# The order of the first tile's work, of the sampled rows' loads and of the last sigmoid in a one-layer decoder kernel

## The reference

```
xn = rms_norm(x, norm_mix_g)                       # x * rsqrt(mean(x^2) + eps) * g
qa, ka, va, qr, kr, vr, gr, g_a, g_b = split(xn @ w_in)   # w_in: 1024 x 11264
oa = differential attention(qa, ka, va)            # 8 heads, prompt causal; sampled rows with a paged cache
or = retention(qr, kr, vr)                         # 4 heads, keys of 256, values of 512, chunks of 128
m  = sigmoid(g_a + b) * (norm(oa) @ w_pa) + sigmoid(g_b + b) * ((norm(or) * silu(gr)) @ w_pb)
h  = x + m @ w_o
y  = rms_norm(h + (silu(hn @ w_g) * (hn @ w_u)) @ w_down),  hn = rms_norm(h)
```

## Time and profile before

| | us |
|---|---|
| runs shown | 2793.14, 2794.50, 2794.54 |
| median | 2794.5 |
| the profiled execution's own time | 2795.3 |
| its span (first to last instruction) | 2793.4 |
| PE busy | 2750.4 (98%) |
| VectorE, GpSimd, ScalarE busy | 1280.7, 867.7, 719.3 |

### The profile page before, as it was taken

How to read it: one execution, slowest core, us unless ns; L and a number is a source line. 1 busy time by engine, 2 the same in 40 slices (tenths; PEclk the granted TensorE clock), 3 DMA queues, 4 the chain that set the end, 5 groups by cost and what they waited for, 6 DMA issues and landing times.

```text
span 2793.4 us, 41305 instructions
## 1 busy us (share of the span) xinstructions
PE 2750.4 (98%) x16146; PEld 2330.2 (83%) x16146; DVE 1280.7 (46%) x2465; ACT 719.3 (26%) x1518; POOL 867.7 (31%) x700
## 2 busy tenths in 40 slices
PE   7999999999999999999999999999999999999998
PEld 5888877777777778787777789999899999997886
DVE  5441255536556644554444442343375555542224
ACT  4111122225555532222121121011232222221011
POOL 3342522202211222221222233535023444455340
PEclk9999999999999999999999999999999999999999
DMA  4324256553343234456545454243122222244321
GB/s 138 123 79 149 95 191 203 201 180 114 100 131 122 85 124 156 161 183 194 184 159 176 156 200 142 102 148 134 68 88 70 70 81 82 70 154 156 91 60 64
DMA packets 277776, 362.11 MB, mean 130 GB/s; under 512 B 28514, under 2 KB 172514, under 8 KB 277602
## 3 DMA queue, kind: packets, MB, share of 16 engines
q1 hardware_dynamic: 277602, 359.74, 38.9%
HBM read 257.24 MB, written 111.35 MB: 132 GB/s over the span
## 4 chain that ended last, share of the span: by engine, by line
PE 93%; DVE 3%; ACT 2%; DMA 1%; issue 1%; SPq 0%; ACTq 0%; DVEq 0%
PE psum L521 22%; PE psum L1293 14%; PE psum L2647 14%; PE psum L2017 13%; PE psum L546 10%; PE psum L986 3%; PE psum L1012 2%; PE psum L2629 2%; PE psum L2050 2%; PE psum L2063 2%; PE psum L1970 1%; PE psum L2671 1%; PE psum L1407 1%; PE psum L1002 1%; PE psum L2056 1%
## 5 line engine op out<-in xcount | busy, mean ns | idle before, releaser
L351 POOL TENSOR_TENSOR w_h<-stage,ones 128x512 fp32r<-128x512 f32 x268 | 305.0, 1165 | 1347.0 <-PE psum L2017 419.5
L358 POOL TENSOR_TENSOR w_l<-stage,w_h 128x512 fp32r<-128x512 f32 x268 | 355.7, 1354 | 123.4 <-DVE acc L1134 118.7
L521 PE MATMUL psum<-w_h,xt_h 128*128 128x512 f32 x864 | 344.4, 399 | 5.9 <-DVE xt_l L492 3.1
L521 PE MATMUL psum<-w_h,xt_l 128*128 128x512 f32 x864 | 343.1, 397 | 0.0
L521 PE MATMUL psum<-w_l,xt_h 128*128 128x512 f32 x864 | 343.0, 397 | 0.0
L2017 PE MATMUL psum<-xt_h,w_h 128*128 128x384 f32 x744 | 289.1, 389 | 0.0
L2017 PE MATMUL psum<-xt_h,w_l 128*128 128x384 f32 x744 | 245.1, 329 | 0.0
L2017 PE MATMUL psum<-xt_l,w_h 128*128 128x384 f32 x744 | 245.0, 329 | 0.0
L401 POOL TENSOR_TENSOR w_l<-stage,w_h 128x512 fp32r<-128x512 f32 x106 | 139.2, 1313 | 268.6 <-ACT w_h L2741 268.6
L1293 PE MATMUL psum<-w_h,xt_h 128*128 128x512 f32 x512 | 218.0, 426 | 0.0
L1293 PE MATMUL psum<-w_l,xt_h 128*128 128x512 f32 x512 | 202.2, 395 | 0.0
(11 more groups left out here) (299 smaller groups left out, 5585.0 us busy)
## 6 DMA issues: line engine op xcount, KB each, us to landing
stage<-in_w_in_dram SPq DMA_DIRECT2D x88, 512.0 KB, 5.7
proj<-edge SPq DMA_DIRECT2D x112, 256.0 KB, 2.0
out_dram<-acc SPq DMA_DIRECT2D x44, 512.0 KB, 3.6
stage<-in_w_gu_dram SPq DMA_DIRECT2D x88, 256.0 KB, 3.8
acc<-proj SPq DMA_DIRECT2D x82, 256.0 KB, 3.1
gates<-edge SPq DMA_DIRECT2D x32, 544.0 KB, 4.1
acc<-in_cache_k_dram SPq DMA_DIRECT2D x32, 512.0 KB, 5.3
acc<-in_cache_v_dram SPq DMA_DIRECT2D x32, 512.0 KB, 4.6
```

Of the source, the lines that this page charges most:

```text
L351: last = nc.gpsimd.tensor_tensor(w_h[s][:, a:b, :], src, one.unsqueeze(1).to_broadcast([128, b - a, WN]), ALU.mult)
L358: last = nc.gpsimd.tensor_tensor(w_l[s][:, a:b, :], stage[h][:, a - lo:b - lo, :], w_h[s][:, a:b, :].bitcast(F), ALU.subtract)
L521: last = nc.tensor.matmul(psum[:, bank, :], x, w[s][:, k, :], start=k == 0 and n == 0, stop=k == nk - 1 and n == len(passes) - 1)
```

## The change

At the start, gain and identity are loaded ahead of the first weight half. VectorE makes the low pieces 5, 6 and 7 of the first weight tile (`BY_DVE`), counted on v_done, and GpSimd the other five. ScalarE makes the first half of rows 0's high part, w_h piece 0, the second half, and the other pieces. From row tile 3 on, square and root (ScalarE) and roots (VectorE) stand ahead of high and low part of the tile before. SP's loads of q and k for head 0 move to step 61 of the attention, behind a wait for the transposes of the last query half; PE waits for those two (32), VectorE for all five (80). `DN_PART` gives ScalarE and VectorE one row tile behind the second chunk instead of three; the others follow the last sigmoid, and VectorE's low parts stand `t + 3` ahead.

```diff
--- before.py
+++ after.py
@@ -114,7 +114,7 @@
 def v_step(n, name):
-    return sum(len(v_names(m)) for m in range(n)) + v_names(n).index(name) + 1
+    return len(BY_DVE) + sum(len(v_names(m)) for m in range(n)) + v_names(n).index(name) + 1
 def s_step(n, name):
@@ -124,7 +124,7 @@
 N_OPERANDS = operand(PAIRS)
-DN_PART = [(0, 2), (2, 5), (5, NT)]
+DN_PART = [(0, 2), (2, 3), (3, NT)]
 LAST_ORDER = [*range(NT - 2), SAMPLE, NT - 2]
@@ -133,12 +133,15 @@
     return banks_before(w) + (LAST_ORDER.index(t) if w == N_W - 1 else t)
-PIECES = 2 * KD - 4
+BY_DVE = [5, 6, 7]
+PIECES = 2 * KD - len(BY_DVE) - 4
 def split_count(w, h):
-    return KD * w + 4 * (h + 1) if w < 2 else PIECES + 2 * w + h + 1
+    if w == 0:
+        return 4 * (h + 1) - (len(BY_DVE) if h else 0)
+    return KD - len(BY_DVE) + 4 * (h + 1) if w == 1 else PIECES + 2 * w + h + 1
 def tile_no(w):
@@ -305,6 +308,8 @@
             sp.wait_ge(op_split, N_OPERANDS)
         elif w >= 1:
             sp.wait_ge(w_split, split_count(tile_no(w) - 1, h))
+            if (w, h) == (1, 1):
+                sp.wait_ge(v_done, len(BY_DVE))
         load_half(sp, w_source(w), h, W_NK[w])
     def load_w(sp, w):
@@ -351,7 +356,7 @@
                     last = nc.gpsimd.tensor_tensor(w_h[s][:, a:b, :], src, one.unsqueeze(1).to_broadcast([128, b - a, WN]),
                                                    ALU.mult)
                 last.then_inc(w_high, 1)
-                pool.wait_ge(w_high, no * 2 + (PIECES + h + 1))
+                pool.wait_ge(w_high, no * 2 + (2 * KD - 4 + h + 1))
                 for a, b in pairs:
                     if beat is not None:
                         pool.wait_ge(mix_ready, beat + (8 * h + 4 + a - lo) * 13 // 16 + 1)
@@ -366,6 +371,8 @@
         def first_low(w):
             for k in range(KD):
+                if w == 0 and k in BY_DVE:
+                    continue
                 pool.wait_ge(w_high, KD * w + k + 1)
                 nc.gpsimd.tensor_tensor(w_l[w][:, k, :], stage[k // 4][:, k % 4, :], w_h[w][:, k, :].bitcast(F),
                                         ALU.subtract).then_inc(w_split, 1)
@@ -472,8 +479,8 @@
     def transposed(tag, g, t):
         return psum[:, norm_banks[tag][2](g), :].rearrange("p (k n) -> p k n", k=4)[:, :, 0:rows(t)]
-    def act_high_tile(act, tag, t, place, xh, xs):
-        for b in range(2):
+    def act_high_tile(act, tag, t, place, xh, xs, bs=range(2)):
+        for b in bs:
             g = place(b)
             act.wait_ge(norm_banks[tag][0], g + 1)
             if t == SAMPLE:
@@ -506,7 +513,9 @@
             for k in ks:
                 if inside is not None and (t, k) in inside:
                     pe_norm_tile(pe, "mix", inside[t, k], lambda b: 2 * inside[t, k] + b)
-                if t == 0 and (pieces or k % 4 == 0):
+                if t == 0 and pieces and split == 1 and k in BY_DVE:
+                    pe.wait_ge(v_done, BY_DVE.index(k) + 1)
+                elif t == 0 and (pieces or k % 4 == 0):
                     pe.wait_ge(w_split, split + (k if pieces else k // 4))
                 state = ready(t, k) if ready is not None else None
                 if state is not None:
@@ -571,9 +580,9 @@
             sp.dma_start(x_rows[0:rows(t), t, :], token_rows(x_prompt, x_sample, t)).then_inc(x_loaded[x_group(t)], 16)
         load_x(0)
+        sp_load_gain(sp, norm_mix_g[0])
+        sp.dma_start(ident[:, :], c_ident).then_inc(ident_loaded, 16)
         load_half(sp, w_source(0), 0)
-        sp.dma_start(ident[:, :], c_ident).then_inc(ident_loaded, 16)
-        sp_load_gain(sp, norm_mix_g[0])
         load_half(sp, w_source(0), 1)
         for t in range(1, NT):
             load_x(t)
@@ -640,7 +649,7 @@
         inside = {(0, 7): 1, (1, 4): 2, (2, 2): 3, (2, 7): 4, (3, 4): 5, (4, 1): 6, (4, 6): 7, (5, 4): 8}
         for j in range(2):
-            pe_token_tile(pe, xt_h1, xt_l1, xs_hl1, j, KD * j + 1, lambda t: (G_TM + NT * j + t, (G_TM + NT * j + t) % RING),
+            pe_token_tile(pe, xt_h1, xt_l1, xs_hl1, j, (KD - len(BY_DVE)) * j + 1, lambda t: (G_TM + NT * j + t, (G_TM + NT * j + t) % RING),
                           ready=None if j else lambda t, k: (mix_free, 2 + 2 * t + k // 4 + 1) if k % 4 == 0 else None,
                           pieces=True, inside=None if j else inside)
         with pe.Fori(1, W_KR // 2) as i:
@@ -660,18 +669,24 @@
             act.wait_ge(x_loaded[x_group(t)], X_GROUPS[x_group(t)] * 16)
             act_square(act, "mix", x_rows, t)
-        def high_tile(t):
-            act_high_tile(act, "mix", t, lambda b: 2 * t + b, xt_h1, xs_hl1)
+        def high_tile(t, bs=range(2)):
+            act_high_tile(act, "mix", t, lambda b: 2 * t + b, xt_h1, xs_hl1, bs)
         act.wait_ge(ones_set, 2)
         nc.scalar.activation(rstd[:, 0:1], ones[:, :], ACT.Sqrt)
         square(0)
         act_deviation(act, "mix", 0)
-        first_high(0, range(KD))
+        high_tile(0, [0])
+        first_high(0, [0])
+        high_tile(0, [1])
+        first_high(0, range(1, KD))
         for t in range(1, NT):
-            high_tile(t - 1)
+            if t == 2:
+                high_tile(t - 1)
             square(t)
             act_deviation(act, "mix", t)
+            if t > 2:
+                high_tile(t - 1)
             if 4 <= t < 8:
                 first_high(1, [2 * (t - 4), 2 * (t - 4) + 1])
         high_tile(NT - 1)
@@ -707,11 +722,18 @@
             dve_low_tile(dve, "mix", t, lambda b: 2 * t + b, xt_h1, xt_l1, xs_hl1)
         for t in range(NT):
-            if t:
+            if 1 <= t <= 2:
                 low_tile(t - 1)
+            if t == 1:
+                for k in BY_DVE:
+                    dve.wait_ge(w_high, k + 1)
+                    nc.vector.tensor_tensor(w_l[0][:, k, :], stage[1][:, k - 4, :], w_h[0][:, k, :].bitcast(F),
+                                            ALU.subtract).then_inc(v_done, 1)
             dve_rstd(dve, "mix", t)
             if t == 0:
                 dve.wait_ge(gain_loaded, 16)
+            if t > 2:
+                low_tile(t - 1)
             dve_scale_tile(dve, "mix", x_rows, t)
         dve_att_constants(dve)
         low_tile(NT - 1)
@@ -936,6 +958,9 @@
                 load_w_half(sp, W_VR + n // 16 + 2, 0 if n % 16 == 8 else 1)
             if n % 3 == 2 and n // 3 < 2 * NT:
                 copy_rows(n // 3)
+            if n == STEPS - 3:
+                sp.wait_ge(x_full, x_index(X_LOADS[-1]) + 1)
+                sp_load_qk_inputs(sp, 0)
         store_half(2 * DH - 2)
         for n in (STEPS - 2, STEPS - 1, STEPS):
             for u in UNITS_OF[n]:
@@ -944,7 +969,7 @@
         for s in range(3):
             sp.wait_ge(stored[s], 16 * (1 + (W_VR + 1) * NT // 3))
         sp.wait_ge(out_read, STEPS)
-        sp.wait_ge(x_full, len(X_ORDER) - 1)
+        sp.wait_ge(n_loaded, 32)
         sp_load_inputs(sp, 0)
         store_half(2 * DH - 1)
@@ -1744,11 +1769,14 @@
     def sample_rows(x, i):
         return x[i * RV:(i + 1) * RV, TP:T].rearrange("(b e) n -> e b n", e=128)
-    def sp_load_inputs(sp, i):
+    def sp_load_qk_inputs(sp, i):
         sp.wait_ge(ns_ready, 2 * DB * i)
         for x, col in ((nq_in, QR), (nk_in, KR)):
             sp.dma_start(x, proj[TP:T, i * RK + col:(i + 1) * RK + col]).then_inc(n_loaded, 16)
+
+    def sp_load_inputs(sp, i):
+
         sp.dma_start(n_decay, c_ret_new[i]).then_inc(n_loaded, 16)
         sp.dma_start(n_qdec, c_ret_qdec[i]).then_inc(n_loaded, 16)
         sp.dma_start(nv_in, proj[TP:T, i * RV + VR:(i + 1) * RV + VR]).then_inc(n_loaded, 16)
@@ -1863,6 +1891,7 @@
                         wait_gates(i)
                         sp.dma_start(nr_gate, sample_rows(gates, i)).then_inc(ng_loaded, 16)
                     if row % 8 == 7 and x == 3 and i + 1 < RH:
+                        sp_load_qk_inputs(sp, i + 1)
                         sp_load_inputs(sp, i + 1)
                     if row % 8 == 7 and x == 11:
                         sp.wait_ge(n_ready, i + 1)
@@ -1932,7 +1961,7 @@
             g, r = divmod(row, 4)
             i, m = divmod(row, 8)
             if (m, x) == (0, 12):
-                pe.wait_ge(n_loaded, 80 * (i + 1))
+                pe.wait_ge(n_loaded, 80 * (i + 1) if i else 32)
                 pe.wait_ge(n_ready, i)
                 for src, a in ((nq_in, 0), (nk_in, KT)):
                     for b in range(KT):
@@ -2219,6 +2248,7 @@
             i, m = divmod(row, 8)
             if (m, x) == (0, 16):
                 dve.wait_ge(nt_read, i + 1)
+                dve.wait_ge(n_loaded, 80 * (i + 1))
                 dve.wait_ge(nr_full, 2 * i)
                 for b in range(KT):
                     for h in range(2):
@@ -3030,8 +3060,8 @@
         for w in range(W_DN, N_W):
             c, n = divmod(w - W_DN, 2)
             for t in LAST_ORDER if w == N_W - 1 else range(NT):
-                if c == 0 and n == 0 and t + 5 < NT:
-                    low(0, t + 5)
+                if c == 0 and n == 0 and t + 3 < NT:
```

(1 more changed line is left out.)

## The result

Four runs of the changed kernel have a median of 2776.8 us (2776.55 to 2780.18), four of the kernel before 2793.8 (2792.39 to 2794.54). The ratio is 0.9942 with a 95% interval of 0.9929 to 0.9956: 17.0 us, 0.6%. The forecast was 2776.4. The profiled execution of the changed kernel is the longest of its four, 2780.2 us around a span of 2778.4; one of the experiments takes a second profile of the same kernel, and it is needed to read this one rightly.

What follows compares the result with a forecast made beforehand. PE, busy 2750.4 of 2793.4 us, was taken as the bound, so only its waits and the slow clock behind them could go. 8.7 + 4.7 + 4.4 = 17.8 us, plus 0.3 for matmul tails, gave 2776.4; range 2771 to 2785.

Steps and rivals of the forecast that it cites:

- The start: Up to the norm's second turn: earlier gain moves tile 2 up 1.0 us, bounded by the landing of rows 2 to 8.
- The turns: Norm, tile 2 to sampled rows: PE becomes the bound, 27.6 us against 34.8, so 7.2 us go.
- The slow clock behind the sampled rows: Behind the norm's wait before the sampled rows: slow matmuls go with the wait, 1.3 us gained.
- The wait for the bank: At tile 6: PE arrives before ScalarE frees the first of six banks, a new wait costing 0.8 us.
- The first tile: Sum of start, turns, clock behind the sampled rows and bank wait: 8.7 us gained, bounds 5.0 to 10.6.
- rival (1): Norm and gates: new waits at tile 2 with slow clock, 5 us turns, gates' bank wait; 2780 to 2783 us, chance 0.13.
- Sampled rows: Transposes of sampled q and k: 3.1 us of wait and 2.2 of slow clock go, net 4.7 us.
- The new wait of 0.6 in the third block: Third gate block: PE waits 0.6 us for the bank that ScalarE frees.
- The last sigmoid: Before the first down matmul: 2.8 us of wait and 1.6 of slow clock go, 4.4 us.
- Rival (2): Down projection: second weights come late by 9 us or more, costing the 4.4; 2781 us, chance 0.04.
- (3): First tile: clock stays at 1.2 GHz through all the norm's turns, slower than before, 2805 us; chance 0.03.
- (4): Early loads or new piece counts make a queue wait where it did not; 0 to 5 us left, 2790; chance 0.04.

Runs made afterwards that it cites:

- the fastest kernel: The changed kernel with rows 2 on their own semaphore, all eight low pieces on GpSimd, square and roots ahead from row tile 2: 2773.9 us.
- two tiles between: The changed kernel with two row tiles of the down projection behind the second chunk instead of one, low parts t + 4 ahead: 2776.9 us.

## Why the prediction was right

The time came out 0.4 us from the forecast by the median, and the shifts change at the places that were named, with the exceptions told of below. By its steps:

- **The start.** Scaling at 6.80 (7.1 predicted), first transposes at 8.18 (8.4), first matmul at 12.10 (12), VectorE free of its pieces at 18.4 (18.5), tile 1 at 20.91 (21.3). The rows' landing as the next bound held: the square ran at 24.21, and of the term of **1.0 us** 0.63 and 0.88 were measured. The three pieces took 4.71 us, between the 2.0 and the 6.0 reckoned, and their end came where I had put it. By the rule of the Trainium skill (SBUF — State Buffer, Who interferes with whom) the end at 20 was to be the likelier one; the trace has 18.4, nearer the middle, since VectorE waited each time for the rest of a GpSimd piece and not for a whole one.
- **The turns.** With the full clock, tile 2 to the sampled rows took 27.71 us (27.75 to 55.46), and 27.6 were worked out from PE's own pieces: 7.07 of the **7.2 us**. PE is the bound there, and no turn waits.
- **The slow clock behind the sampled rows.** 1.4 us against **1.3**, in both profiles. It is a cost that not every execution of the old order pays: with the sampled rows' inputs alone and with the start alone the wait was there (2.28 and 2.30 us) and the clock stayed at 1.00. The wait for the bank: 0.5 us, **-0.6** in the shifts against -0.8.
- **The term that was mis-sized.** The first tile was to give 8.7 us. It gives 8.76 in the second profile and 6.91 in the first. Of the 1.8 between them 1.6 arise from tile 2 to tile 3 (0.63 to -0.63 in the table, where the second profile goes from 0.88 to 1.19): the slow clock behind the wait at tile 2, the half of rival (1) that came in one of two profiles of the same kernel. The wait of 1.5 to 2 us stood in that rival's own text with a chance of 0.13; on what the runs show, the forecast should have carried it as a cost of 1.6 us that some executions pay.
- **Sampled rows.** 3.2 of wait and 2.1 of clock were measured for **3.1 and 2.2**. The new wait of 0.6 in the third block was about 0.2: PE reached it after 2.8 us from the transposes, where I had reckoned 2.3, and the bank was free after 2.7 (2.9 reckoned). 5.3 for **4.7**.
- **The last sigmoid.** 3.0 and 1.6 for **2.8 and 1.6**: 4.6 for **4.4**. The price came as worked out. The next weights are issued 15.0 us behind the first down matmul (14.8 predicted, 4.35 before), GpSimd's halves are done 15.3 us before PE turns to them (2549.8 less 2534.5) and, with 12 matmuls of 0.233 between, 9.0 (2552.6 less 2543.6): the 15 and 9 of the prediction. Rival (2) is out.
- **What was in no term.** Three things lie outside the three places, and no edit is there. Between 70 and 325 us PE's matmuls are closer together in the second profile of the changed kernel than in its first and in the kernel before: 1.1 us, told of below. Behind the first down weights the shift falls by 1.1 us in both profiles. Near 1595 us PE waits 0.9 us for VectorE in the profile before and in both of the changed kernel, and in the first profile of the changed kernel alone the clock falls behind it:

```profile
1595.20:1598.40 3.20, 3.20 (x13) 3.20 (x13) 0.74 (x2) 0.53 (x1) 0.00 (x0) 0.50 0.59 220
```

That costs 1.6 us, of which 0.9 come back, since a later wait (0.7 us before) is gone. In the second profile that later wait is 1.4 us, and 0.8 are lost.
- **The other rivals.** (3) and (4) did not come. From 35 us to the end of the first tile the clock is 1.00; the one stretch of matmuls at 1.2 GHz after that is the one at 1595 us. No queue waits where it did not.

That the sum was right to 0.4 us is partly luck. With the full clock the three places give 8.8 + 5.3 + 4.6 = 18.7 us for 18.1; the closer matmuls add 1.1, and 0.8 and 1.1 are lost, which leaves 17.9. With the slow stretch at tile 2 it is 6.9 + 5.3 + 4.6 = 16.8, less 0.7 and 1.1: 15.0. The medians, 17.0 and 16.7, lie between.

## What to carry to other kernels

Where one engine is busy 98% of the time, the worth of a removed wait is the wait and, when the clock fell behind it, the slow matmuls as well: here 3.2 + 2.1 and 3.0 + 1.6. Put the row-wise square and root of the next tile ahead of this tile's wide copies on both engines, so that the chain of small steps lies beside the transposes; this alone gave 7.6 us here, of the 17 of the whole change. A start that is pulled forward is worth only what the next load allows, so look at which semaphore the next tile shares before paying for an earlier first matmul: 4.2 us at the first matmul were 0.6 to 0.9 at the third tile, and one more semaphore gave 1.4 more there. Before a gain of 1 us in one profile is explained, profile the same kernel a second time.

## What the hardware showed that I had not expected

- Whether the clock falls behind a wait isn't settled by the length of the wait. At tile 2, with nearly the same work ahead of it, it fell behind 1.89 and 2.00 us and stayed at 1.00 behind 1.65, 1.77 and 2.39 us. Before the sampled rows' transposes it fell behind 2.29 us in the kernel before and in the one with the sigmoid alone, and stayed at 1.00 behind 2.28 and 2.30 us with the sampled rows' inputs alone and with the start alone, though the same 196 matmuls and transposes ran ahead of it. Near 1595 us the changed kernel waited 0.9 us in both of its profiles, and the clock fell to 0.50 in one and stayed at 1.00 in the other. So the slow matmuls behind one such wait are a cost that some executions pay and others don't.
- VectorE beside GpSimd: in the start of the fastest kernel the last product of the root, one column, takes 1.02 us for 0.16 alone and ends at 18.26, where a GpSimd piece ends at 18.25; another step of one column takes 0.57 for 0.22 and ends at 17.02, a piece at 17.01. So the surcharge isn't a fixed one: it is what is left of the GpSimd piece that is running, here 0.4 to 1.0 us, whatever the size of VectorE's instruction, and a chain of small steps is the dearest beside GpSimd. Steps with one operand from SBUF (0.15 us) pay nothing, and neither does the low part of the rows, whose one operand lies in PSUM (0.68 to 0.69 us beside GpSimd and alone). GpSimd pays too: the piece beside the scaling of 2.28 us (1.28 alone) takes 2.27 for 1.3. The Trainium skill (SBUF — State Buffer, Who interferes with whom) states such a lock, for a VectorE instruction with two SBUF inputs beside a GpSimd instruction that reads SBUF; these rows agree.
- PE's matmuls of 512 columns have two paces, 0.2333 and 0.2324 us apart, with the granted clock at 1.00 and no wait in both. Between 70 and 325 us the pace is the slower one in the kernel before, the changed kernel's first profile, the sigmoid alone and the changed kernel without VectorE's pieces, and the faster one in the other nine profiles, the second of the changed kernel among them (256.67 and 255.62 us for the same 1100 matmuls). One kernel had both, so there it is a matter of the execution. In the down projection it is the faster one before, with the roots alone, with the start alone and with two tiles between, and the slower one in the other nine (86.45 and 86.80 us for the same 372 matmuls, 1.1 us over the whole of it). The cause is open and wasn't tried, so 1 us between two single profiles proves nothing.
